# Causal mask of two attention units: added by VectorE in PSUM in place of two TensorE products

## The chip, the cores and the metric

The kernel runs on one core of a Trainium2 chip. The metric is the device time of one execution in microseconds (us). The median of three runs of the kernel before is 3585.42 us; the runs lie between 3579.69 and 3586.85.

## The reference

The program is two blocks of a network in float32, one after the other, on 512 tokens of width 1024. The first has two layers; each is a feed-forward part, a token mixer, and another feed-forward part. The mixer runs three kinds of attention side by side, all causal over blocks of 128 queries:

```python
s = jnp.einsum('bqhd,bkhd->bhqk', qn, k_nope) + ...          # mla: 4 heads
s = jnp.where(kpos[None, :] <= qpos[:, None], s, NEG)         # NEG = -1e30
p = jax.nn.softmax(s, axis=-1)
a = p[:, :, 0] - lam * p[:, :, 1]                             # diff: 4 heads, 2 maps each
o = gt[..., 0:1] * o_cmp + gt[..., 1:2] * o_slc + gt[..., 2:3] * o_win   # nsa: 8 heads
```

With 512 tokens the selected and the windowed attention of nsa both see all keys up to the query, so each of their maps is a plain causal softmax. The compressed attention has 31 keys and a mask of its own. The second block (retention, gated linear attention and two feed-forward parts) has no part in the change.

## The kernel before

Everything is written out by hand: one instruction stream for each of TensorE (`pe`), VectorE (`dve`), ScalarE (`act`), GpSimd (`pool`) and SyncE (`sp`), in the order of the code, with semaphores between them. A `signal` counts events of one kind; `x.wait_ge(*name(layer, n))` waits for the n-th.

Attention of a layer is 4 query tiles of 128 rows, handled in the order `TILE_AT = (3, 0, 2, 1)`. Tile 3 looks at four key tiles (512 keys), tile 0 at one, tile 2 at three, tile 1 at two. A tile has `UN` = 14 units, and a unit is two maps: 2 mla units, 4 diff units, 8 nsa units. So a layer has `NU` = 56 units and 112 maps. Each engine's `attention` runs over t, with i the place of the tile and `step` the unit in it. Work of several units overlaps: in round t,

- TensorE writes the scores of unit t (L3365) to two PSUM banks, one for each map. Two pairs of banks are used in turn, so it first waits for the exponentials of unit t-2. In diff and nsa units the two maps lie in different rows of the array; mla maps use 96 rows and come one after the other. Then it adds the mask: for each map one bf16 product of the identity `ident_b` with the triangle `causal_b` (0 or -1e30), accumulated on the last 128 columns (L3367). The event `scores_done` follows. Then come the transposes of the probabilities of unit t-3 (L3396), and the products of unit t-4 with the values (L3430 for the compressed part, L3437 for the rest).
- VectorE takes the maximum of both maps at once, negated, over all n columns (L2409, `max_ready`). It then copies the second transposed map of unit t-3 out of PSUM (L2418), and takes the reciprocal of the sums of unit t-1 (L2423).
- ScalarE copies the first transposed map of unit t-3 (L1448), waits for the maximum, and writes the exponentials of unit t with their sums (L1458).
- GpSimd scales the probabilities of a unit by the reciprocals (L958 to L962).

Some steps of each tile have more. At step 1 TensorE adds the compressed scores (L3375), and VectorE masks them and starts their softmax (`cmp_softmax`: L2362, L2366, L2368). At step 2 ScalarE takes their exponentials (L1464) and VectorE their sums (`cmp_sums`: L2374 to L2381). At step 6 their transposes follow (L3403). At steps 10 and 11 the diff outputs leave PSUM (L2442, L2443). In 18 of the 56 rounds TensorE also runs a piece of the second block's modulation, a product with `ada_w` (L3460). VectorE copies its rows at the end of the round (L2450), TensorE turns them in the next round behind the masks and before the transposes (L3383), and VectorE adds them to `mod` behind the reciprocal (L2428).

TensorE, VectorE and ScalarE each wait in order, so an instruction that waits holds up all behind it on its engine. `causal_b` is made once from `causal` and lies in SBUF.

Of the kernel before, what the change touches and what calls it, by code (L numbers as in the profile page):

```python
# [10 lines left out]
ALU = mybir.AluOpType  # L11
# [196 lines left out]
def build(nc, a, out):  # L208
    ctx = ExitStack()
    with ctx:  # L210
# [14 lines left out]
        def signal(name, per_layer, start=0):  # L225
            return Signal(sem(name), per_layer, start)
# [300 lines left out]
        gate_exp = signal("gate_exp", 1)  # L527
        gate_step = signal("gate_step", 2)
        scores_done = signal("scores_done", NU + TT)
        max_ready = signal("max_ready", NU)  # L530
        exp_ready = signal("exp_ready", NU)
        probs_turned = signal("probs_turned", 2 * NU)
        probs_t_act = signal("probs_t_act", NU)
# [493 lines left out]
        def _(act):  # L1027
# [403 lines left out]
            def attention(layer):  # L1431
# [6 lines left out]
                for t in range(NU + X_LAG):  # L1438
# [9 lines left out]
                        nc.scalar.activation(probs_t[u % 2][:, 0, 0:n], psum[:, 4, 0:n], ACT.Copy).then_inc(probs_t_act.sem, 1)  # L1448
                    if t < NU:

                        act.wait_ge(*max_ready(layer, t + 1))
                        tile = TILE_AT[i]
                        n = (tile + 1) * P
                        for m in range(2):
                            if m and u >= 0:

                                act.wait_ge(*probs_turned(layer, 2 * u + 2))
                            last = nc.scalar.activation(probs[:, t % 3, m, 0:n], psum[:, score_banks(t) + m, 0:n], ACT.Exp,  # L1458
                                                        bias=neg_max[:, 2 * t + m:2 * t + m + 1], accum_out=exp_sum[:, 2 * t + m:2 * t + m + 1])
                        last.then_inc(exp_ready.sem, 1)  # L1460
                        at = slice(tile * P, (tile + 1) * P)
                        if step == AT_CMP_EXP:
                            act.wait_ge(*cmp_step(layer, 2 + 7 * i + 3))
                            nc.scalar.activation(cmp_p[:, :, 0:NC], cmp_p[:, :, 0:NC], ACT.Exp).then_inc(cmp_exp.sem, 1)  # L1464
                        if step == AT_LAST and i:
                            last_high(i - 1)
                        if step == AT_FIRST:
                            act.wait_ge(*o_done(layer, i * UN + FIRST_NSA))
                            if i:

                                act.wait_ge(*diff_sum(layer, i))
                            nc.scalar.activation(diff_sq, psum[:, 6, 2 * P:4 * P], ACT.Square).then_inc(diff_squared.sem, 1)
                            nc.scalar.activation(h_hi[:, 0:2, at], psum[:, 6, 0:2 * P].rearrange("p (c q) -> p c q", c=2),
                                                 ACT.Copy).then_inc(o_hi_ready.sem, 1)
                        if step == AT_SUMS:
                            act.wait_ge(*diff_sum(layer, i + 1))
                            nc.scalar.activation(diff_sums(tile), psum[:, 6, 0:2 * P],
                                                 ACT.Copy, scale=-1.0).then_inc(diff_moved.sem, 1)
# [387 lines left out]
        def _(dve):  # L1866
# [525 lines left out]
            def attention(layer):  # L2392
# [11 lines left out]
                for t in range(NU + O_LAG + 1):  # L2404
                    i, step = divmod(t, UN)
                    if t < NU:
                        b = score_banks(t)
                        dve.wait_ge(*unit_scores_done(layer, t))
                        nc.vector.tensor_reduce(neg_max[:, 2 * t:2 * t + 2], psum[:, b:b + 2, 0:(TILE_AT[i] + 1) * P], AX_X, ALU.max,  # L2409
                                                negate=True).then_inc(max_ready.sem, 1)  # L2410
                    u = t - X_LAG
                    if 0 <= u < NU:
                        dve.wait_ge(*probs_turned(layer, 2 * u + 2))
# [494 lines left out]
        def _(pe):  # L2908
# [437 lines left out]
            def attention(layer):  # L3346
# [7 lines left out]
                for t in range(NU + O_LAG + 1):  # L3354
                    i, step = divmod(t, UN)
                    if t < NU:
                        if t >= 2:

                            pe.wait_ge(*exp_ready(layer, t - 1))
                        tile = TILE_AT[i]  # L3360
                        n = (tile + 1) * P
                        banks = [psum[:, score_banks(t) + m, :] for m in range(2)]
                        for m, head in enumerate(UNIT_MAPS[step]):
                            q, k, _ = key_values(*head)
                            nc.tensor.matmul(banks[m][:, 0:n], q(slice(tile * P, (tile + 1) * P)), k(n), start=True, stop=False)  # L3365
                        for m in range(2):
                            last = nc.tensor.matmul(banks[m][:, n - P:n], ident_b[:], causal_b[:], start=False, stop=True)  # L3367
                        last.then_inc(scores_done.sem, 1)
                        if step == AT_CMP:
                            if i:  # L3370

                                pe.wait_ge(*diff_moved(layer, i))
                                pe.wait_ge(*ada_read(layer, 2 * sum(at < t - 1 for at in ADA_STEPS)))
                            for c in range(NSA_H // NSA_G):
                                last = nc.tensor.matmul(psum[:, 6, 2 * c * CMP_BLOCK:2 * c * CMP_BLOCK + NSA_G * NC], q_nsa[:, c, tile * P:(tile + 1) * P],  # L3375
                                                        k_cmp[:].rearrange("p g n -> p (g n)"), start=True, stop=True)
                            last.then_inc(scores_done.sem, 1)
# [579 lines left out]
```

## Time and profile before

| | us |
|---|---|
| median of 3 runs | 3585.42 |
| runs | 3585.42, 3586.85, 3579.69 |
| span of the profiled execution | 3577.6 |
| TensorE busy | 3496.6 (98%) |
| TensorE weight loads busy | 2932.5 (82%) |
| VectorE busy | 1683.2 (47%) |
| ScalarE busy | 1484.3 (41%) |
| GpSimd busy | 1522.5 (43%) |
| masks (L3367) | 224 products per execution, 217 to 314 ns each |
| maxima (L2409) | 112, from 414 to 1226 ns |

The profile shows one execution. Its span runs from the first to the last instruction of the program, and a run's time lies some microseconds above it. PE is TensorE's products, PEld its weight loads, DVE is VectorE, ACT ScalarE, POOL GpSimd and SP SyncE. Products overlap each other, so each record is longer than the distance to the next, and a busy TensorE isn't one at its peak; the starts are what tells its pace. An arrow in a row names what ended an engine's idle time.

### The profile page before, as it was taken

The numbers are of one execution on the slowest core, as the hardware profiler recorded it, in microseconds if no ns is written. First come the engines' busy times: TensorE is split into PE (matmuls) and PEld (weight loads), VectorE is DVE, ScalarE is ACT, GpSimd is POOL, SyncE is SP. The second block draws the span as 40 slices with busy tenths as digits, with TensorE's granted clock in tenths as the row PEclk, the third lists the DMA queues.
The fourth block names the chain that finished last, engine by engine and source line by source line (L and its number), as shares of the span: only waits on it lengthen the run. The fifth ranks groups of instructions, "written<-read, shape, count | busy, mean of one in ns | idle before, by whom it ended". The sixth has DMA issues, their size and how long they took to land.

```text
span 3577.6 us, 56728 instructions
## 1 busy us (share of the span) xinstructions
PE 3496.6 (98%) x21603; PEld 2932.5 (82%) x21603; DVE 1683.2 (47%) x2814; ACT 1484.3 (41%) x2466; POOL 1522.5 (43%) x1352
## 2 busy tenths in 40 slices
PE   8999999999999999999999999999999999999998
PEld 7999776688998999776689997888888786778887
DVE  8456635575657565644575656211112504661112
ACT  5344434554545454534554545312112325443223
POOL 4555543445455554543435554323233532034443
PEclk9999999999999999999999999999999999999999
DMA  4343443323333343433314333222212323013332
GB/s 124 105 113 89 113 121 107 101 60 106 106 92 97 106 111 90 98 117 121 117 49 118 86 103 100 65 65 59 65 58 60 90 64 88 30 55 98 100 94 65
DMA packets 569573, 322.63 MB, mean 90 GB/s; under 512 B 30282, under 2 KB 563376, under 8 KB 569008
## 3 DMA queue, kind: packets, MB, share of 16 engines
q1 hardware_dynamic: 569392, 320.22, 31.4%
q8 instruction: 113, 1.85, 0.2%
q14 instruction: 68, 0.56, 0.1%
HBM read 318.08 MB, written 2.10 MB: 89 GB/s over the span
## 4 chain that ended last, share of the span: by engine, by line
PE 65%; issue 21%; POOL 8%; DVE 3%; ACT 1%; POOLq 0%; ACTq 0%; DVEq 0%
PE psum L3052 21%; PE psum L2945 16%; PE psum L3159 12%; POOL w_lo L945 7%; PE psum L3365 2%; PE psum L3437 2%; PE psum L3396 2%; PE psum L3339 1%; PE psum L3086 1%; PE psum L3089 1%; PE psum L3460 1%; PE psum L3206 1%; PE psum L3476 1%; PE psum L3367 1%; POOL set_lo L996 0%
## 5 line engine op out<-in xcount | busy, mean ns | idle before, releaser
L945 POOL TENSOR_TENSOR w_lo<-w_raw,w_hi 128x512 fp32r<-128x512 f32 x488 | 656.0, 1367 | 1107.9 <-ACT w_hi L1033 1107.9
L1033 ACT ACTIVATE w_hi<-w_raw 128x1024 fp32r<-128x1024 f32 x244 | 257.6, 1058 | 842.3 <-PE psum L2945 714.6
L2945 PE MATMUL psum<-h_hi,w_hi 128*128 128x512 f32 x1136 | 454.5, 400 | 1.4 <-POOL w_lo L945 1.4
L2945 PE MATMUL psum<-h_hi,w_lo 128*128 128x512 f32 x1136 | 447.2, 394 | 0.0
L2945 PE MATMUL psum<-h_lo,w_hi 128*128 128x512 f32 x1136 | 444.3, 391 | 0.0
L996 POOL TENSOR_TENSOR set_lo<-w_raw,set_hi 128x512 fp32r<-128x512 f32 x224 | 292.6, 1334 | 225.3 <-ACT set_hi L1112 222.3
L3052 PE MATMUL psum<-t_hi,set_hi 128*128 128x256 f32 x1280 | 363.4, 284 | 10.1 <-ACT gated L1102 8.2
L3052 PE MATMUL psum<-t_lo,set_hi 128*128 128x256 f32 x1280 | 362.4, 283 | 0.0
L3052 PE MATMUL psum<-t_hi,set_lo 128*128 128x256 f32 x1280 | 362.3, 283 | 0.0
L3159 PE MATMUL psum<-a_hi,set_hi 128*128 128x512 f32 x704 | 277.0, 393 | 2.8 <-DVE a_lo L2096 2.8
L3052 PE MATMUL psum<-b_hi,set_hi 128*128 128x256 f32 x960 | 272.6, 284 | 1.8 <-DVE gated L2168 1.8
L3159 PE MATMUL psum<-a_lo,set_hi 128*128 128x512 f32 x704 | 274.1, 389 | 0.0
L3159 PE MATMUL psum<-a_hi,set_lo 128*128 128x512 f32 x704 | 274.0, 389 | 0.0
L3052 PE MATMUL psum<-b_lo,set_hi 128*128 128x256 f32 x960 | 272.2, 284 | 0.0
L3052 PE MATMUL psum<-b_hi,set_lo 128*128 128x256 f32 x960 | 272.2, 284 | 0.0
L2945 PEld LDWEIGHTS psum<-h_hi,w_hi 128*128 128x128 f32 x1136 | 213.3, 188 | 60.5 <-issue 10.9
L978 POOL TENSOR_TENSOR set_lo<-w_raw,set_hi 128x512 fp32r<-128x512 f32 x160 | 212.6, 1349 | 114.9 <-ACT set_hi L1089 108.0
L2062 DVE TENSOR_TENSOR gated<-silu_g,psum 128x512 f32<-128x512 f32 x66 | 37.6, 597 | 474.8 <-ACT silu_g L1157 474.8
L984 POOL TENSOR_TENSOR set_lo<-w_raw,set_hi 128x512 fp32r<-128x512 f32 x160 | 210.9, 1339 | 114.8 <-ACT set_hi L1092 114.8
L3052 PEld LDWEIGHTS psum<-t_hi,set_hi 128*128 128x128 f32 x1280 | 245.8, 192 | 12.0 <-POOL set_lo L978 8.1
L2945 PEld LDWEIGHTS psum<-h_lo,w_hi 128*128 128x128 f32 x1136 | 213.3, 188 | 50.3 <-issue 4.3
L2945 PEld LDWEIGHTS psum<-h_hi,w_lo 128*128 128x128 f32 x1136 | 213.3, 188 | 45.9
(626 smaller groups left out, 8085.8 us busy)
## 6 DMA issues: line engine op xcount, KB each, us to landing
w_raw<-ffn_w SPq DMA_DIRECT2D x120, 512.0 KB, 3.8
w_raw<-ffn_w_gate SPq DMA_DIRECT2D x88, 512.0 KB, 4.0
w_raw<-ffn_w_up SPq DMA_DIRECT2D x88, 512.0 KB, 3.9
ada_raw<-ada_w SPq DMA_DIRECT2D x72, 512.0 KB, 4.7
w_raw<-ffn_w_down SPq DMA_DIRECT2D x64, 512.0 KB, 4.1
w_raw<-w_in SPq DMA_DIRECT2D x60, 512.0 KB, 3.8
w_raw<-ffn_w_down SPq DMA_DIRECT2D x32, 384.0 KB, 3.6
w_raw<-w_out SPq DMA_DIRECT2D x24, 512.0 KB, 4.1
```

Source lines behind the costliest of these rows:

```text
L945: last = nc.gpsimd.tensor_tensor(w_lo[:, i, at], w_raw[:, i, at], w_hi[:, i, at].bitcast(F32), ALU.subtract)
L978: last = nc.gpsimd.tensor_tensor(lo[:, at], w_raw[:, 2 * r, at], hi[:, at].bitcast(F32), ALU.subtract)
L984: last = nc.gpsimd.tensor_tensor(lo[:, to], w_raw[:, 2 * r + 1, at], hi[:, to].bitcast(F32), ALU.subtract)
L996: last = nc.gpsimd.tensor_tensor(set_lo[i // 2][:, to], w_raw[:, i, at], set_hi[i // 2][:, to].bitcast(F32), ALU.subtract)
L1033: nc.scalar.activation(w_hi[:, pos, :], w_raw[:, pos, :], ACT.Copy).then_inc(hi_ready, 1)
L2062: last = nc.vector.tensor_tensor(gated[:, i, o:o + n], silu_g[:, i, o:o + n], up, ALU.mult)
L2945: last = nc.tensor.matmul(dst, w[:, pos, k * P:(k + 1) * P], rhs[g][r](k0 + k), start=k == 0 and m == 0, stop=k == nk - 1 and m == 2)
L3052: last = nc.tensor.matmul(dst, w[r][:, at], x[:, k, cols], start=not onto and k == 0 and m == 0, stop=k == HALF_K - 1 and m == 2, skip_gro ...
L3159: last = nc.tensor.matmul(psum[:, 6 + i % 2, :], w[i // 2][:, at], x[:, k, :], start=k == m == 0, stop=k == nf - 1 and m == 2)
L3365: nc.tensor.matmul(banks[m][:, 0:n], q(slice(tile * P, (tile + 1) * P)), k(n), start=True, stop=False)
L3396: last = nc.tensor.transpose(psum[:, 4 + m, b * P:(b + 1) * P], probs[:, u % 3, m, b * P:(b + 1) * P], ident[:])
L3437: last = nc.tensor.matmul(o_place(kind, h), v(b), probs_t[u % 2][:, x, b * P:(b + 1) * P], start=first and b == 0, stop=final and b == TIL ...
```

## The change

For each unit VectorE adds the triangle to the last 128 columns of both banks in one instruction (128 partitions x 256 elements, `causal_b` repeated for both), reading and writing PSUM. It then waits for that result and takes the maximum. The events of both are counted in one signal, `max_step`, two for each unit; ScalarE waits for the second. TensorE no longer multiplies the identity with the triangle, and the scores of a map are one closed product. There are 112 additions more on VectorE, and 224 products and as many weight loads fewer on TensorE.

```diff
-        max_ready = signal("max_ready", NU)
+        max_step = signal("max_step", 2 * NU)
 ...
-                        act.wait_ge(*max_ready(layer, t + 1))
+                        act.wait_ge(*max_step(layer, 2 * t + 2))
 ...
                     if t < NU:
                         b = score_banks(t)
+                        n = (TILE_AT[i] + 1) * P
                         dve.wait_ge(*unit_scores_done(layer, t))
-                        nc.vector.tensor_reduce(neg_max[:, 2 * t:2 * t + 2], psum[:, b:b + 2, 0:(TILE_AT[i] + 1) * P], AX_X, ALU.max,
-                                                negate=True).then_inc(max_ready.sem, 1)
+                        diagonal = psum[:, b:b + 2, n - P:n]
+                        nc.vector.tensor_tensor(diagonal, diagonal, causal_b[:].rearrange("p (o k) -> p o k", o=1).broadcast_to([P, 2, P]),
+                                                ALU.add).then_inc(max_step.sem, 1)
+                        dve.wait_ge(*max_step(layer, 2 * t + 1))
+                        nc.vector.tensor_reduce(neg_max[:, 2 * t:2 * t + 2], psum[:, b:b + 2, 0:n], AX_X, ALU.max,
+                                                negate=True).then_inc(max_step.sem, 1)
 ...
                             q, k, _ = key_values(*head)
-                            nc.tensor.matmul(banks[m][:, 0:n], q(slice(tile * P, (tile + 1) * P)), k(n), start=True, stop=False)
-                        for m in range(2):
-                            last = nc.tensor.matmul(banks[m][:, n - P:n], ident_b[:], causal_b[:], start=False, stop=True)
+                            last = nc.tensor.matmul(banks[m][:, 0:n], q(slice(tile * P, (tile + 1) * P)), k(n), start=True, stop=True)
                         last.then_inc(scores_done.sem, 1)
```

## Rows read from the trace of the kernel before

**Rows 1.** The page, first part: busy time, share of the span, instructions.

```profile
PE 3496.6 (98%) x21603; PEld 2932.5 (82%) x21603; DVE 1683.2 (47%) x2814; ACT 1484.3 (41%) x2466; POOL 1522.5 (43%) x1352
```

**Rows 2.** Busy time by stretches: length, PE, PEld, DVE, ACT, POOL, clock, DMA, GB/s.

```profile
540.60:722.50 181.90, 172.68 (x1657) 111.85 (x1657) 98.30 (x251) 92.79 (x301) 71.92 (x118) 0.95 0.32 101
```

**Rows 3.** Waits of PE, 538 to 724 us: us in total, times, longest us.

```profile
PE psum L3430 <- DVE probs_t L2418: 2.4, 3, 0.9
PE psum L3437 <- DVE mod L2428: 2.2, 3, 0.9
PE psum L3383 <- DVE diff_rows L2450: 2.0, 2, 1.5
```

**Rows 4.** Timeline of PE: start us, us, line, operands, count [idle <- releaser].

```profile
545.49 0.28 PE L3367 MATMUL psum<-causal_b,ident_b 128*128 128x128 bf16 x2
545.60 1.05 PE L3375 MATMUL psum<-k_cmp,q_nsa 128*128 128x62 f32 x8
...
714.65 0.28 PE L3367 MATMUL psum<-causal_b,ident_b 128*128 128x128 bf16 x2
714.77 0.61 PE L3396 MATMUL psum<-ident,probs 128*128 128x128 f32 x4
...
719.41 0.66 PE L3396 MATMUL psum<-ident,probs 128*128 128x128 f32 x4
```

**Rows 5.** Single lines of DVE: count, ns min/median/max, first and last start, forms.

```profile
L2443 DVE TENSOR_TENSOR h_lo<-psum,h_hi x8: 414/415/415, 588.1 to 1795.6; 128x256 fp32r<-128x256 f32 x8
...
L2368 DVE TENSOR_TENSOR cmp_p<-cmp_p,cmp_stats x8: 416/506/864, 548.1 to 1769.7; 128x248 f32<-128x248 f32 x8
...
L2103 DVE TENSOR_TENSOR silu<-psum,silu x40: 414/425/426, 58.8 to 2153.9; 128x256 f32<-128x256 f32 x40
```

**Rows 6.** Timeline of DVE, tile 0.

```profile
622.20 0.42 DVE L2409 TENSOR_REDUCE neg_max<-psum 128x2 f32<-128x256 f32 x1 [0.58 <-PE psum L3367]
622.54 0.28 DVE L2418 COPY probs_t<-psum 128x128 f32<-128x128 f32 x1
...
623.43 0.42 DVE L2409 TENSOR_REDUCE neg_max<-psum 128x2 f32<-128x256 f32 x1 [0.54 <-PE psum L3367]
```

**Rows 7.** Timeline of DVE, steps 1 to 4 of tile 2.

```profile
638.41 0.41 DVE L2366 TENSOR_REDUCE cmp_stats<-cmp_p 128x8 f32<-128x248 f32 x1
638.85 0.42 DVE L2368 TENSOR_TENSOR cmp_p<-cmp_p,cmp_stats 128x248 f32<-128x248 f32 x1
639.19 0.95 DVE L2409 TENSOR_REDUCE neg_max<-psum 128x2 f32<-128x768 f32 x1
...
642.70 0.95 DVE L2409 TENSOR_REDUCE neg_max<-psum 128x2 f32<-128x768 f32 x1
...
644.11 0.40 DVE L2450 COPY diff_rows<-psum 128x256 f32<-128x256 f32 x1
...
645.92 0.56 DVE L2418 COPY probs_t<-psum 128x384 f32<-128x384 f32 x1 [0.55 <-PE psum L3396]
```

**Rows 8.** Timeline of ACT and PE: last exponential of a unit, scores two units on.

```profile
631.52 0.20 ACT L1458 ACTIVATION_READ_ACCUMULATOR probs<-psum,neg_max 128x1 f32 x1
...
632.39 0.91 PE L3365 MATMUL psum<-k_mla,q_mla 96*128 96x384 f32 x2
```

**Rows 9.** Timeline of PE, step 4 of tile 2.

```profile
644.57 0.61 PE L3383 MATMUL psum<-cond_sum,diff_rows 128*128 128x2 f32 x4 [0.57 <-DVE diff_rows L2450]
```

**Rows 10.** Timeline of DVE, step 2 of tile 3.

```profile
548.90 1.21 DVE L2409 TENSOR_REDUCE neg_max<-psum 128x2 f32<-128x1024 f32 x1
```

**Rows 11.** Timeline of DVE and PE, steps 3 and 4 of tile 1.

```profile
691.08 0.42 DVE L2450 COPY diff_rows<-psum 128x256 f32<-128x256 f32 x1 [0.35 <-PE psum L3460]
...
691.70 0.45 PE L3383 MATMUL psum<-cond_sum,diff_rows 128*128 128x2 f32 x3
```

**Rows 12.** Busy time by stretches, as rows 2: two stretches at half clock.

```profile
552.00:562.20 10.20, 8.83 (x46) 6.33 (x50) 5.16 (x12) 3.87 (x10) 2.58 (x4) 0.50 0.18 56
613.40:620.20 6.80, 6.56 (x43) 3.15 (x42) 2.84 (x9) 2.13 (x10) 2.18 (x5) 0.50 0.25 79
```

## The prediction, made before the changed kernel had run

> **What bounds the kernel now.** The page comes first: TensorE is busy 98% of the span [rows 1]. The change lies in two stretches, one per layer, between the first score matmul of attention and the first matmul of the output projection. The table by stretches gives 181.9 us for the first, with TensorE busy 172.7 and VectorE 98.3 [rows 2]; the second is as long. Then I read what TensorE waits for inside the first stretch: for VectorE in three places, 2.4 us in three waits behind the first transposes of the turn (L3430), 2.2 us in three waits before L3437, 2.0 us in two waits before L3383 [rows 3]. So TensorE sets the pace of most of the 56 units of a layer, and VectorE does so at a few fixed places. A saving on TensorE counts only in the first kind, a longer VectorE only in the second. These are read apart below.
>
> **Part 1, TensorE loses two bf16 matmuls a unit.** In a plain unit of two key tiles the masks start at 714.65 and the transposes behind them at 714.77: 0.12 us [rows 4]. That isn't all profit. Behind the masks the four transposes span 0.61 us, because their first weight load ran under a mask. At 719.41, where they follow matmuls that use the array in halves, as the scores of the diff and nsa units do, they span 0.66 [rows 4]. Without masks the transposes stand right behind such scores. So I take 0.12 - 0.05 = 0.07 us for a diff or nsa unit. In an mla unit the scores take turns on the whole array, the next weight load is prefetched anyway, and the masks cost all of 545.49 to 545.60, 0.11 us [rows 4]. Bounds: 0.12 for all (no exposed load), and zero (the pipe has to drain there whoever comes next).
>
> **Which units give it.** A layer has 8 mla and 48 other units. Units in which TensorE waits for VectorE give nothing: steps 1 to 3 of the first tile handled (queries of tile 3), 1 to 4 of the third (tile 2) and 1 to 4 of the fourth (tile 1), plus about two more at steps 10 and 11. That leaves 5 mla and 38 others: 5 x 0.11 + 38 x 0.07 = 3.2 us a layer.
>
> **Part 2, VectorE gets an add of 128x256 from and to PSUM, and a wait on itself.** The trace has no such add that writes to PSUM. Nearest is the subtraction at L2443, one input in PSUM, one in SBUF, the same size: 414 to 415 ns in all 8 [rows 5]. The wait costs more than it seems. Where nothing waits, the next instruction starts before the last has ended: the maximum at 622.20 takes 0.42 and the copy behind it starts at 622.54, after 0.34 [rows 6]. Where it waits for its predecessor's result, 638.41 with 0.41 is followed at 638.85, after 0.44 [rows 7]. I take 0.45 us from the start of the add to the start of the maximum. Bounds: 0.34 (no wait), and 0.86, the longest run of L2368, an instruction of about this size [rows 5]. Against that, the add can start before the masks would have ended: 0.22 us earlier (two masks of 0.28 us span, of which 0.06 passes while the scores drain) behind packed scores, 0.11 behind mla ones. The maximum then comes later by 0.45 - 0.22 = 0.23 us, or 0.34 in an mla unit.
>
> The Trainium skill ("VectorE: DVE Perf Modes", the section on the DRAIN) states that a semaphore after each VectorE instruction costs nothing extra over one after the last. By that rule the add costs 0.34, and the gain of the sum below would be 3.4 us instead of 1.5. The trace disagrees, with 0.44 against 0.34 between starts [rows 6, 7], so I go by the rows.
>
> **Where the later maximum is covered.** Queued behind it on VectorE are the copy of probs_t, the reciprocal, the ada add and copy. Who waits: ScalarE's exponential for the maximum, TensorE's transposes and outputs for the copy, GpSimd for the reciprocal. In most units the copy (L2418) waits for TensorE's transposes and not for the maximum: 645.92, after 0.55 us of idling [rows 7]. The exponential must end before the scores two units later; in about the tightest case they end at 631.72 and the scores start at 632.39, 0.67 left for 0.23 [rows 8]. In the narrow tile 0 (one key tile) the maxima stand 1.23 us apart, of which VectorE idles 0.54 [rows 6] and works 0.7. With the add it works 1.15 of some 1.17. That just fits, and is the thinnest cover here.
>
> **Where it isn't.** After step 1 of a tile VectorE does the compressed-attention softmax in one chain: maximum, softmax, maximum of step 2, exponentials, sums, maximum of step 3, copy of ada rows (L2450), for which TensorE's L3383 waits.
> - Tile 2: the maximum at 639.19 stands directly behind L2368, that at 642.70 behind the sums, the copy at 644.11 behind them [rows 7], and L3383 starts at 644.57 after idling 0.57 [rows 9]. Three adds lie in it; the first has a slack of 0.24 for its 0.34, so 0.10 + 0.45 + 0.45 = 1.0 us. The next add, behind that copy, fits the 0.55 before the copy.
> - Tile 3: the maximum of step 1 and that of step 2, at 548.90 right behind the softmax [rows 10], are in the chain of the 1.5 us wait [rows 3]: 0.34 + 0.45 = 0.79.
> - Tile 1: TensorE doesn't wait now; the copy starts at 691.08 after 0.35 of idling, ends at 691.50, and L3383 starts at 691.70 [rows 11], slack 0.20 + 0.35. Two adds, 0.90, less these 0.55: 0.35.
> - Tile 0: its ada copy waits for TensorE far longer than two adds take, and covers them.
> - Small: the wait for L2443 at step 11 of tile 3, 0.15; at the end the last unit's scaling on GpSimd, 0.2.
>
> **The sum.** 1.0 + 0.79 + 0.35 + 0.35 = 2.5 us lost per layer, 3.2 saved: 0.7 net, some 1.5 us for both. The profiled span is 3577.6; the median of the runs is 3585.4, 7.8 above it, the runs lie between 3579.7 and 3586.9, so what lies around the span is 2 to 9 us. 3577.6 - 1.5 = 3576.1 for the span, and the same step from the median gives 3583.9 us. A large edit, 448 instructions gone from TensorE, that nearly cancels.
>
> **Rivals.**
> 1. The masks' whole 0.12 us is won in every unit and the waits swallow nothing: 112 x 0.12 = 13.4 us, 3572; with today's waiting units left out 10 us, 3575. For it: TensorE's 98%. Against it: [rows 3], and 0.61 against 0.66 in [rows 4].
> 2. Slower: the add contends with GpSimd's scaling of probabilities for SBUF, in the same stretch. L2368 takes 416 to 864 ns [rows 5]; each add would take 0.44 us more. Per layer: 0.9 in tile 3, 1.3 each in tiles 2 and 1, 1.5 around steps 10 and 16 to 17, and 2.2 in the five back-to-back units of tile 0, where nothing covers it: some 7.3, 15 for both, 3585.4 - 1.5 + 15 = 3599 us. It decides from 0.26 us more per add ((7.2 + 1.5) / 15 x 0.44). Against it: L2103, PSUM with SBUF and the same size, stays at 414 to 426 ns in 40 instructions through stretches full of GpSimd work [rows 5].
> 3. The half clock. TensorE ran at half clock from 552.0 to 562.2 and from 613.4 to 620.2 in the first layer [rows 12], and once in the second; the first follows the waits at steps 2 and 3. One stretch of 6.8 us in which TensorE is busy 6.56 costs half of that, 3.3 us. The change adds 1.0 us and takes away the work of four units' masks just before L3383 in tile 2, so TensorE would idle 0.57 + 1.0 + 0.25 = 1.8 us there, as much as before the first stretch. One such stretch in each layer: +6.6 - 1.5, 3590.5. Three or more would be needed for slower by 0.2%. On the other side the one of 613.4 may vanish: 3580. The Trainium skill ("TensorE: Matmul & The Clock Gate", HAM oscillation) has the clock fall when waits break up the matmuls; by that rule these stretches come with longer waits, which is this rival.
> 4. The change doesn't do what it says: TensorE has to drain between scores and transposes, and the masks lay in that time. Nothing is saved and the 5 us of waits are paid: 3590.
>
> **Chances.** Forecast 0.48 (about 3580 to 3587), rival 1 0.16, rival 2 0.07, rival 3 with more half clock 0.13 and with less 0.08, rival 4 0.08. 0.2%, 7.2 us, is about what a measurement of this kernel can tell from no change: faster means under 3578.2, slower over 3592.6. Faster: rival 1 and a little of the others, 0.18. Slower: rival 2 and the far part of rival 3, plus chains longer than I see, 0.15. Within: 0.67. The range takes in the full mask saving with waits (3575) and more half clock with rival 4 (3594): 3574 to 3594.
>
> **What would show it.** Transposes start 0.00 to 0.01 us after the scores' last pass and the four of them span 0.66; the distance from the first score to the first score of the next unit shrinks by 0.07 in plain units (tiles 3, 2 and 1). The add takes 0.41 to 0.43 us, the maximum starts 0.45 after it. The waits of TensorE for L2450 grow from 2 to about 5 us per layer in tiles 3, 2 and 1; those before L3430 and L3437 stay at 0.6 to 0.95. The stretches of attention come out at 181 us each. I am wrong if the add takes over 0.5 us, if the plain units shrink by 0.12, or if the granted clock differs.

## The result, and the profile after

| | before | after |
|---|---|---|
| median, us | 3583.41 (9 runs, 3578.23 to 3586.85) | 3598.87 (9 runs, 3587.15 to 3603.66) |
| span of the profiled execution, us | 3577.6 | 3594.6 |
| mean granted clock in it | 0.993 | 0.987 |

The ratio is 1.0037, with a 95% interval of 1.0026 to 1.0048. The changed kernel is slower by 15.5 us, where 1.5 us less was forecast, and it lies outside the stated range of 3574 to 3594.

The page of the changed kernel, its busy times and the row of the clock over 40 slices of the span:

```profile
PE 3506.2 (98%) x21379; PEld 2930.0 (82%) x21379; DVE 1726.4 (48%) x2926; ACT 1486.8 (41%) x2466; POOL 1525.4 (42%) x1352
...
PEclk9999998999999999999899999999999999999999
```

Against [rows 1], TensorE has 224 instructions fewer and yet 9.6 us more busy time. That can't be its work. The clock row (the mean granted clock of each slice, in tenths) shows an 8 in two slices, and each lies in one of the two attention stretches. In the kernel before there is a 9 everywhere.

Busy time by stretches of the changed kernel (start:end, length, PE, PEld, DVE, ACT, POOL, clock, DMA share, GB/s; a clock of 0.50 is the lower of TensorE's two levels, 1.2 against 2.4 GHz, called half clock here): the first layer's attention, from its first score to the output projection, and four stretches in it.

```profile
538.50:730.00 191.50, 178.62 (x1545) 112.32 (x1546) 120.24 (x307) 93.99 (x301) 72.62 (x118) 0.89 0.30 95
549.80:560.00 10.20, 8.55 (x40) 6.07 (x40) 6.09 (x14) 4.16 (x11) 2.53 (x5) 0.50 0.19 62
611.20:624.90 13.70, 13.27 (x82) 6.77 (x78) 6.51 (x24) 4.94 (x25) 4.42 (x10) 0.50 0.30 98
628.30:638.50 10.20, 10.12 (x44) 5.27 (x45) 4.34 (x16) 3.81 (x17) 2.65 (x6) 0.50 0.04 13
652.20:659.00 6.80, 6.80 (x48) 3.93 (x44) 2.71 (x5) 2.32 (x8) 2.74 (x5) 0.50 0.01 2
```

The stretch that took 181.9 us at a clock of 0.95 [rows 2] takes 191.5 at 0.89, and that of the second layer 191.0 at 0.90; 181 each was forecast. The kernel before had two stretches at half clock in it, 10.2 and 6.8 us [rows 12]. Now there are four: 10.2 us in tile 3 as before, 13.7 us where 6.8 stood in tile 0, and two new ones, 10.2 us at the passage from tile 0 to tile 2 and 6.8 us in tile 2. In the second layer half-clock stretches in attention grew from 6.8 us to 37.5 (6.8, 13.7, 10.2 and 6.8). Over the whole profiled execution they add up to 97.8 us, against 54.7 before; attention has 78.4 of them, against 23.8. From the first score to the last unit's first score the two layers took 175.5 and 172.1 us before and take 184.8 and 184.0 now, 21.1 us more. Taken from unit to unit, these 21.1 us stand in ten units of each layer, those under the new or longer stretches: steps 5 to 9 of tile 0, its steps 11 to 13 with step 0 of tile 2, and step 5 of tile 2. They take 21.4 us more, and the 90 other distances together 0.3 less.

What TensorE waits for in the same stretch (us in total, times, longest us):

```profile
PE psum L3386 <- DVE diff_rows L2455: 5.0, 3, 2.5
PE psum L3433 <- DVE probs_t L2423: 2.5, 3, 1.0
PE psum L3440 <- DVE mod L2433: 2.2, 3, 0.9
```

These answer to [rows 3]. The wait for the copied ada rows grew from 2.0 to 5.0 us; the two others stay. The timeline of VectorE, then of TensorE, at steps 3 and 4 of tile 2:

```profile
647.33 0.42 DVE L2411 TENSOR_TENSOR psum<-psum,causal_b 128x256 f32<-128x256 f32 x1
647.79 0.96 DVE L2414 TENSOR_REDUCE neg_max<-psum 128x2 f32<-128x768 f32 x1
648.67 0.55 DVE L2423 COPY probs_t<-psum 128x384 f32<-128x384 f32 x1
649.13 0.15 DVE L2428 RECIPROCAL scaled_inv<-exp_sum 128x2 f32<-128x2 f32 x1
649.21 0.40 DVE L2455 COPY diff_rows<-psum 128x256 f32<-128x256 f32 x1
...
649.66 0.61 PE L3386 MATMUL psum<-cond_sum,diff_rows 128*128 128x2 f32 x4 [1.88 <-DVE diff_rows L2455]
```

The add stands in the chain, the maximum starts 0.46 us behind it, and TensorE idles 1.88 us where it idled 0.57 [rows 9]. The same wait in tile 3 is 2.5 us, and in tile 1 there is a new one of 0.56.

Two plain units of tile 1, TensorE in the kernel before, then TensorE and VectorE in the changed one:

```profile
714.02 0.70 PE L3365 MATMUL psum<-k_slc,q_nsa 64*128 64x256 f32 x4
...
716.12 0.70 PE L3365 MATMUL psum<-k_win,q_nsa 64*128 64x256 f32 x4
...
721.24 0.70 PE L3370 MATMUL psum<-k_slc,q_nsa 64*128 64x256 f32 x4
721.88 0.66 PE L3399 MATMUL psum<-ident,probs 128*128 128x128 f32 x4
...
723.27 0.70 PE L3370 MATMUL psum<-k_win,q_nsa 64*128 64x256 f32 x4
...
721.99 0.43 DVE L2411 TENSOR_TENSOR psum<-psum,causal_b 128x256 f32<-128x256 f32 x1 [0.76 <-PE psum L3370]
722.46 0.69 DVE L2414 TENSOR_REDUCE neg_max<-psum 128x2 f32<-128x512 f32 x1
```

The transposes follow the scores directly and span 0.66 us, and the distance from score to score is 2.03 us. It was 2.10 in the kernel before, from 714.02 to 716.12.

### The profile page after: what moved, and what is told of

Read it like the earlier page. It is cut to its first block, busy times and chain, and to the rows that moved or that the text cites. A ratio compares the mean times of both kernels' runs of the same rounds, so it can differ in the third digit from the quotient of the medians.

```text
span 3594.6 us, 56392 instructions
## 1 busy us (share of the span) xinstructions
PE 3506.2 (98%) x21379; PEld 2930.0 (82%) x21379; DVE 1726.4 (48%) x2926; ACT 1486.8 (41%) x2466; POOL 1525.4 (42%) x1352
## 4 chain that ended last, share of the span: by engine, by line
PE 64%; issue 22%; POOL 8%; DVE 3%; ACT 1%; POOLq 0%; ACTq 0%; DVEq 0%
PE psum L3057 21%; PE psum L2950 16%; PE psum L3164 12%; POOL w_lo L945 7%; PE psum L3370 2%; PE psum L3440 2%; PE psum L3399 2%; PE psum L3344 1%; PE psum L3463 1%; PE psum L3091 1%; PE psum L3094 1%; PE psum L3211 1%; PE psum L3479 1%; PE psum L3386 0%; POOL set_lo L996 0%
## 5 line engine op out<-in xcount | busy, mean ns | idle before, releaser
L2062 DVE TENSOR_TENSOR gated<-silu_g,psum 128x512 f32<-128x512 f32 x66 | 37.5, 596 | 474.8 <-ACT silu_g L1157 474.8
```

What stands on the lines that cost most here:

```text
L2062: last = nc.vector.tensor_tensor(gated[:, i, o:o + n], silu_g[:, i, o:o + n], up, ALU.mult)
```

## How the clock is taken apart from the rest

A single run's time swings with its clock, so I give each run two numbers: its time, and its half-clock time, (1 - mean clock) x 2 x span. The mean clock has three digits, which makes steps of 7 us. The changed kernel has 101 us of half clock in the median (79 to 115), the kernel before 64 (36 to 79, 98 runs beside the experiments, median time 3583.5). This number covers the whole execution: in the 14 profiled ones 19 to 46 us of it lie outside attention.

A least-squares fit through all 223 runs of all kernels below, with one level for each kernel and one common slope, leaves a scatter of 1.4 us. Its slope is 0.37 us of time for 1 us at half clock. The last column of the table is the kernel's level against the kernel before: what it would cost or gain if the clock were the same (uncertain by about 0.5 us, the scatter over the root of the runs). The four groups of runs of the kernel before, taken beside the experiments on three chips, differ by up to 1.1 us by the same reckoning, so differences of 1 us between kernels of different groups mean little. The limit of 90 us in the table was chosen after the runs were seen.

| kernel | runs | median, us | ratio to before (95%) | half clock, us | runs over 90 us of it | at equal clock, us |
|---|---|---|---|---|---|---|
| before | 98 | 3583.5 | | 64 | 0 | 0 |
| after | 9 | 3598.9 | 1.0037 (1.0026 to 1.0048) | 101 | 7 | +0.1 |
| e1_both | 10 | 3591.4 | 1.0025 (1.0015 to 1.0035) | 65 | 0 | +8.4 |
| e2_neither | 10 | 3578.1 | 0.9986 (0.9976 to 0.9996) | 72 | 1 | -7.6 |
| e3_tile0_on_pe | 10 | 3586.9 | 1.0006 (0.9997 to 1.0016) | 79 | 0 | -0.1 |
| e4_mixed | 10 | 3579.0 | 0.9992 (0.9981 to 1.0002) | 64 | 0 | -4.7 |
| e5_tile0_twice | 10 | 3588.6 | 1.0013 (1.0003 to 1.0023) | 72 | 0 | +0.9 |
| e6_tile0_bare | 10 | 3589.8 | 1.0017 (1.0007 to 1.0027) | 83 | 4 | -1.0 |
| e7_filled_waits | 10 | 3581.2 | 1.0003 (0.9983 to 1.0024) | 64 | 3 | -1.6 |
| e9_before_filled | 10 | 3576.4 | 0.9978 (0.9966 to 0.9991) | 46 | 0 | -0.6 |
| e10_fill_tile2 | 10 | 3587.4 | 1.0021 (1.0001 to 1.0040) | 86 | 4 | -2.5 |
| e11_fill_tile3 | 10 | 3582.5 | 0.9999 (0.9986 to 1.0012) | 64 | 1 | -1.2 |
| e8 and e12 together | 16 | 3572.8 | (each for itself, below) | 50 | 0 | -4.8 |

The theory after the result: the sum of waits and savings is right, and the loss is half clock. Its rival: the adds cost more than they seem to in some place, and the clock only goes along with it.

## Experiments: the two halves of the change

The diffs are shortened to two functions: `adds(t)` says whether VectorE adds the mask of unit t, and `products(t)` whether TensorE forms its mask products. In the changed kernel they are True and False.

**e1_both.** TensorE's products stay, VectorE adds as well.

```diff
-    products(t): return False
+    products(t): return True
```

> TensorE keeps its two mask products in every unit and VectorE adds the triangle as well (masked twice, which changes nothing in the result): the VectorE half of the change alone. Theory A, that the half clock in the narrow tile 0 comes from the two products missing on TensorE: tile 0 goes as in the kernel before (first layer one stretch of half clock or none, not 13.7 + 10.2 us), and only the waits behind VectorE are paid: 3583.4 + 5 = 3588, up to 3595 if the longer wait in tile 2 (step 4) still brings a stretch of half clock in each layer. Theory B, that the half clock comes from VectorE's add, which makes everything behind it later: half clock as in the changed kernel, and the masks' time on top: 3605.

**e2_neither.** Neither of them; the causal mask is left out.

```diff
-    adds(t): return True
+    adds(t): return False
```

> No mask products on TensorE and no add on VectorE: the TensorE half of the change alone (the causal mask of these units is left out, so the result is another). Theory A: half clock in tile 0 of both layers as in the changed kernel (23.9 us of it per layer there), but not the stretch behind step 4 of tile 2, whose wait is short again: 3599 less 5 of waits less 5 to 6 of clock, 3588. Theory B: half clock as in the kernel before, and the saving of 0.07 to 0.15 us a unit counts: 3583.4 - 8.6 = 3575.

Measured: 3591.4 and 3578.1 us. At equal clock the adds alone cost 8.4 us, and the products alone are worth 7.6. e1 came out as theory A had it (3588 to 3595). e2 lies between its two theories (3588 and 3575), nearer to B: with the products gone and nothing added, nine of ten runs stayed at 86 us of half clock or less. In e1 TensorE's wait for the copied rows is 3.7 us in all, longest 1.9. Its half clock is at the level of the kernel before, and in its profiled execution tile 0 has none. The windows (first row tile 0, second row tile 2):

```profile
611.20:624.90 13.70, 12.14 (x126) 7.32 (x122) 9.38 (x33) 7.14 (x34) 5.95 (x14) 1.00 0.57 181
644.30:651.10 6.80, 6.80 (x48) 4.27 (x50) 2.62 (x5) 2.52 (x8) 2.93 (x5) 0.50 0.00 0
```

In the window of tile 0 that ran at 0.50 in the changed kernel the clock is 1.00 here, although VectorE adds there too; tile 2 has its stretch of 6.8 us. In e2, with nothing added, one run in ten fell to 100 us of half clock. It is the profiled one, and it has 13.7 us of it in tile 0:

```profile
611.80:625.50 13.70, 13.28 (x80) 6.94 (x80) 4.66 (x18) 4.39 (x24) 4.36 (x10) 0.50 0.29 88
```

The same 13.7 us stand in its second layer; another 46 us of its 104 lie outside attention. So tile 0 can fall without any add. The two halves sum to +0.8 us; together, in the changed kernel and its three filled versions below, they give +0.1 to -2.5. A likely reason is one that the prediction used: with the products gone the add starts earlier. No run separates it.

**e3_tile0_on_pe.** The change in tiles 3, 2 and 1 only.

```diff
-    adds(t): return True
-    products(t): return False
+    adds(t): return t // UN != 1
+    products(t): return t // UN == 1
```

> The change in tiles 3, 2 and 1; in tile 0 (the second handled, 14 units a layer) the masks stay TensorE products and VectorE adds nothing. Theory A: tile 0 and the start of tile 2 lose their half clock, which cost 4.8 + 1.6 us in the first layer and 7.3 + 1.6 in the second by the distances between scores: 3598.9 - 15 = 3584. The stretch behind step 4 of tile 2 (2.7 us a layer) stays. Theory B, waits of tile 2 and 3 that bring the clock down: little changes, 3595 to 3599.

Measured: 3586.9 us, 79 us of half clock, no run over 79. Theory A had 3584, theory B 3595 to 3599. 12 of the 15 us of the loss are gone with tile 0's change undone, and at equal clock nothing moved (-0.1). Tile 2 still has its stretch (645.0 us, 10.2 us long) behind a wait of 1.9.

**e4_mixed.** As e3, and steps 1 to 3 of every tile also keep the products, so the softmax chain has no add in it. 33 of 56 units add on VectorE.

```diff
+    adds(t): return t // UN != 1 and not 1 <= t % UN <= 3
+    products(t): return not adds(t)
```

> As the one before, and steps 1 to 3 of every tile keep their mask products too, so that VectorE has no add in the chain of the compressed softmax. 33 units of 56 add on VectorE. Theory A, with the waits as a second and separate cost: no half clock beyond that of the kernel before, TensorE's waits for the ada copy back at 2 us a layer, and the saving of 30 x 0.075 + 3 x 0.14 = 2.7 us a layer: 3583.4 - 5.3 = 3578. Theory B (any add brings half clock): 3590 or more.

Measured: 3579.0 us (3578 by theory A), 64 us of half clock, -4.7 at equal clock. The waits for the copied rows and the clock in the window in which tile 2 fell in the changed kernel:

```profile
PE psum L3399 <- DVE diff_rows L2465: 1.7, 2, 0.9
...
644.00:654.00 10.00, 8.78 (x88) 5.79 (x89) 6.93 (x16) 5.55 (x16) 4.73 (x8) 1.00 0.53 169
```

With the wait in tile 2 back to 0.8 us its stretch is gone. But tile 0 fell in this execution (13.7 us from 610.1), with its products in place and no add.

## Experiments: what sends tile 0 down

**e5_tile0_twice.** The change, and in tile 0 the products as well.

```diff
-    products(t): return False
+    products(t): return t // UN == 1
```

> The change as it is in every tile, and in tile 0 TensorE forms the two mask products of a unit as well (the mask is added twice there, which leaves the probabilities as they are). VectorE and its waits are those of the change; TensorE has its 14 x 2 products of tile 0 back. Theory W (tile 0 falls to half clock because work of TensorE is missing there, so that small waits weigh more): tile 0 stays at full clock as in the kernel before, or falls in some runs only; the stretches of tile 2 behind the wait for diff_rows stay as in the changed kernel; half-clock time a run 65 to 80 us, time 3588 +-3 (changed kernel 3599, less 20 to 30 us of half clock at 0.4 us per us). Theory A (it is the add on VectorE that makes tile 0 fall, whatever TensorE does): tile 0 falls as in the changed kernel, half-clock time about 100 us, 3597 to 3601.

**e6_tile0_bare.** The change in tiles 3, 2 and 1; in tile 0 neither, so its causal mask is left out.

```diff
-    adds(t): return True
+    adds(t): return t // UN != 1
```

> The change in tiles 3, 2 and 1; in tile 0 neither the products nor the add (the causal mask of tile 0 is left out, so the result differs there). Theory W: the products are missing as in the changed kernel, so tile 0 falls to half clock in most runs, about 95 to 105 us of half clock a run and 3595 to 3599. Theory A: without the add tile 0 stays at full clock, half-clock time 65 to 80 us and 3586 +-3. A mixture (products gone alone: some runs, as in the kernel without mask and add, where 3 of 10 runs had over 75 us) would give a median at 3586 to 3590 with a wide spread.

Measured: e5 3588.6 us and 72 us of half clock, no run over 86. Theory W gave 3588, theory A 3597 to 3601: the add isn't what makes tile 0 fall. e6 3589.8 us, with runs at 79 to 115 us of half clock, four of ten over 90. That is the mixture named in advance, not W's "most runs". The profiled run of e6 is one of those four, and shows how far a fall can reach:

```profile
612.40:626.10 13.70, 13.45 (x82) 6.76 (x80) 4.85 (x19) 4.83 (x25) 4.42 (x11) 0.50 0.31 100
629.40:666.90 37.50, 36.61 (x174) 20.50 (x174) 16.92 (x46) 13.59 (x48) 10.85 (x19) 0.50 0.10 34
```

The pairs that differ in tile 0's products alone say the same: over 90 us of half clock in 7 of 9 executions of the changed kernel and in 0 of 10 of e5, in 4 of 10 of e6 and 0 of 10 of e3. So does the whole set, 20 of 59 executions of the six kernels without the products in tile 0 (after, e2, e6, e7, e10, e11) and none of 164 of those that have them (before, e1, e3, e4, e5, e8, e9, e12), though these kernels differ in their waits too. The missing products in tile 0 open the way to the executions with much half clock; they don't force one, and e4 shows that a single 13.7 us fall can come with the products in place.

## Experiments: do the waits send the clock down?

These kernels put products that nobody reads into a wait of TensorE, just ahead of it: 128 bf16 columns of the identity with `causal_b`, into bank 4, which is free there. They do nothing but keep TensorE at work.

```diff
+                    if FILL.get(t):
+                        if t > X_LAG:
+                            pe.wait_ge(*first_turn_read(layer, TURN_AT["unit", t - X_LAG] - 1))
+                        for _ in range(FILL[t]):
+                            nc.tensor.matmul(psum[:, 4, 0:P], ident_b[:], causal_b[:], start=True, stop=True)
                     if t - 1 in ADA_AT:
```

**e7_filled_waits.** The change with `FILL = {3: 30, 32: 26}`, tile 3's step 3 and tile 2's step 4.

> The change, with products that nobody reads (128 columns of bf16 into a free bank) in TensorE's two longest waits for diff_rows: 30 of them in tile 3's step 3 (the wait there is 2.5 us) and 26 in tile 2's step 4 (1.9 us), where they end before the awaited rows are there. Nothing else moves. Theory I (the idle stretch itself sends the clock down behind it): the half-clock stretches at 549.8/10.2 us and 652.2/6.8 us, and their two of the second layer, are gone, the half-clock time falls by 20 to 34 us to 65 to 80 us, and the time by 8 to 14 us to 3585 to 3591. If the clock falls for what TensorE does over a longer time, or by something outside of the wait, the stretches stay and the time stays at 3597 to 3601. Tile 0 isn't touched: its stretches stay under theories W and A; only if tile 0's fall follows on tile 3's is it gone too.

Measured: 3581.2 us, 17.6 less than the changed kernel (12.8 between the means), for 56 products a layer that compute nothing. Half clock in the median is 64 us, down from 101. Theory I had 3585 to 3591; the rest of the gain is tile 0's, which fell less often. Against the kernel before it isn't faster (1.0003). The timeline of TensorE at step 3 of tile 3, and the windows of the stretches:

```profile
549.24 1.85 PE L3399 MATMUL psum<-causal_b,ident_b 128*128 128x128 bf16 x30
551.61 0.61 PE L3405 MATMUL psum<-cond_sum,diff_rows 128*128 128x2 f32 x4 [0.53 <-DVE diff_rows L2466]
...
549.80:560.00 10.20, 9.67 (x101) 6.73 (x100) 8.03 (x18) 4.91 (x13) 3.85 (x6) 1.00 0.39 119
610.00:620.20 10.20, 10.20 (x70) 5.32 (x66) 4.23 (x15) 3.28 (x17) 3.17 (x8) 0.50 0.34 104
652.20:659.00 6.80, 6.80 (x69) 4.30 (x67) 4.74 (x12) 3.65 (x11) 2.60 (x4) 1.00 0.50 147
```

The 30 products fill the wait, the awaited rows still come later, and 0.53 us of idling is left. Where the changed kernel ran at 0.50 from 549.8 and from 652.2, this one runs at 1.00. Tile 0 still fell once, in the first layer; the second layer has no half clock in attention at all. Against the rival after the result: that layer has the same adds in tile 0, and steps 6 to 9 take 8.8 us from score to score, where the changed kernel took 13.7 at half clock and the kernel before 8.4. Three of the ten runs have 108 us of half clock, so the tile 0 falls aren't cured.

**e10_fill_tile2** and **e11_fill_tile3.** One fill alone: `FILL = {32: 26}` and `FILL = {3: 30}`.

> The change with only the wait of tile 2's step 4 filled (26 unread products). Theory I: its two stretches of 6.8 us go and nothing else changes: 3599 - 14 x 0.4 = 3593 +-3, half-clock time 87 us, tile 0 (which comes before) as in the changed kernel. If tile 2's stretch was not caused by this wait: 3597 to 3601.

> The change with only the wait of tile 3's step 3 filled (30 unread products). Theory I in its narrow form (a wait reaches only the stretch right behind it): the stretches at 549.8/10.2 and 1648.9/6.8 go, 3599 - 17 x 0.4 = 3592 +-3, tile 0 and tile 2 as in the changed kernel. In a wider form (tile 0 falls because tile 3 fell before it): tile 0's stretches go in many runs as well, half-clock time 50 to 65 us, time 3578 to 3585.

Measured: e10 3587.4 us with 86 us of half clock (87 expected), and the first layer of its profile has the stretches of tiles 3 and 0 as in the changed kernel, while the window of tile 2 runs at full clock:

```profile
549.70:559.90 10.20, 8.51 (x40) 6.07 (x40) 6.09 (x14) 4.20 (x11) 2.54 (x5) 0.50 0.18 58
611.20:624.90 13.70, 13.27 (x82) 6.78 (x79) 6.46 (x24) 4.93 (x24) 4.42 (x10) 0.50 0.28 92
644.00:654.00 10.00, 8.77 (x91) 5.56 (x88) 7.20 (x19) 5.25 (x16) 4.50 (x7) 1.00 0.34 108
```

The time came out 6 us below the 3593 expected. Four of its runs lie at 108 to 122 us of half clock and six at 64 to 86, so a median of ten is a coarse number here. e11 gave 3582.5 us with 64 us of half clock, what the wide form said: only one run of ten went over 90, against seven of nine in the changed kernel. But e7, which has the same fill, had three of ten. Together, over 90 us came in 4 of 20 executions with tile 3's wait filled (e7, e11) and in 11 of 19 without (after, e10). That what happens in tile 3 reaches tile 0, 50 us later, is suggested by this and not settled, and how it would isn't shown. Nor do the falls of tile 3 all vanish: in the profile of e11 one of 6.8 us still stands at 552.5 and one of 3.4 in the second layer.

**e9_before_filled.** The kernel before in its order of work (masks on TensorE), with `FILL = {3: 20}`.

> The kernel before in its order of work (masks on TensorE, none on VectorE) with 20 unread products in its longest wait for diff_rows, tile 3's step 3 (1.5 us in the first layer, 1.8 in the second). If the idle stretch sends the clock down whatever the mask does, the stretches at 552.0/10.2 and 1640.8/6.8 us go: half-clock time 64 - 17 = 47 us, time 3584 - 7 = 3577 +-3, and the changed kernel with its waits filled (3581, median 64 us of half clock) has then to be set beside that. If filling helps only where VectorE adds the mask, it stays at 3584.

Measured: 3576.4 us, ratio 0.9978 (0.9966 to 0.9991), 46 us of half clock, where 3577 and 47 were expected. In its profile the two windows of [rows 12] are at full clock. In the second layer, though, it fell in tiles 0 and 2 (the last two rows), without any wait over 0.9 us close ahead of either:

```profile
552.00:562.20 10.20, 10.20 (x99) 6.50 (x97) 5.74 (x13) 6.00 (x16) 5.12 (x7) 1.00 0.36 115
613.40:620.20 6.80, 5.98 (x66) 3.70 (x64) 3.82 (x15) 4.00 (x19) 2.89 (x7) 1.00 0.72 234
...
1688.50:1695.30 6.80, 6.55 (x42) 3.18 (x40) 2.77 (x9) 2.17 (x10) 2.18 (x5) 0.50 0.22 73
1722.60:1729.40 6.80, 6.80 (x46) 3.62 (x42) 2.28 (x4) 1.90 (x6) 2.38 (x4) 0.50 0.00 0
```

So the mechanism isn't bound to where the mask is added. It was in the kernel before, and the change fed it.

**e8_mixed_filled** and **e12_mixed_again.** e4 with `FILL = {3: 18, 32: 10}`; the same kernel twice.

> The mixed kernel of before (VectorE's add in tiles 3, 2 and 1 but for their steps 1 to 3, TensorE's products elsewhere; 3579.0 us, 64 us of half clock) with unread products in the same two waits, 18 in tile 3's step 3 and 10 in tile 2's step 4. Theory I: the stretch that follows tile 3's step 3 in each layer (10.2 and 6.8 us) is gone, half-clock time about 48 us, time 3579 - 6 = 3573 +-3. If the wait doesn't send the clock down: 3579 as without them, or 1 us more if 18 products reach past the wait.

> The mixed kernel with the two filled waits once more, unchanged, since it was executed only four times and is the fastest so far. If its gain is that of the shorter waits and the stretches that went, it stays at 3569 +-3 with a half-clock time of 29 to 50 us; if the four runs were a lucky draw of tile 0, single runs come at 65 to 80 us of half clock and the median moves to 3573 to 3578. The kernel before stays at 3584.

Measured: e8 3568.6 us in four runs, ratio 0.9950 (0.9933 to 0.9967). e12 3576.5 us in twelve runs on another chip, 0.9992 (0.9979 to 1.0005), half clock from 36 to 86 us. The first was a lucky draw, as e12's second case had it. The sixteen together have a median of 3572.8, between 3567.0 and 3588.4, 10.7 us under the 3583.5 of the kernel before. Beside its own group of the kernel before (3580.8) e12 alone is 4.3 us lower. At equal clock the kernel stands where e4 stands, at -4.8. It is the fastest tried, but only one of its two groups is clear of no change. Of the kernels that compute the whole mask, the one that beats the kernel before with a clear interval in a group of ten is e9.

**All profiled executions together**, two layers of each of 14. The wait is that of TensorE for the copied rows, as it stands or as the fill leaves it:

| | wait, us | layers | with a half-clock stretch behind it |
|---|---|---|---|
| tile 3, step 3, not filled | 0.9 to 2.5 | 18 | 18 (6.8 or 10.2 us) |
| tile 3, step 3, filled | 0 to 0.6 | 10 | 3 (3.4 to 6.8 us) |
| tile 2, step 4, not filled | 1.7 to 1.9 | 11 | 11 (6.8 or 10.2 us) |
| tile 2, step 4, not filled, neither mask nor add (e2) | 0.9 | 2 | 2 |
| tile 2, step 4, short or filled | 0 to 0.8 | 14 | 1 |

Left out is the first layer of e6, whose 37.5 us cover tile 2 already. For tile 2 the question is settled: a wait of 1.7 to 1.9 us sends the clock down, and unread products in it keep it up. A second wait there, 0.87 us for `mod`, comes some 2 us later in all these kernels, and doesn't do it alone.

In tile 3 the wait for the copied rows isn't the only one that counts. Some 2 us ahead of it TensorE waits 0.7 to 2.2 us for the weights `ada_w` from DMA, and in three of the 18 layers (one each of e3, e5 and e10) the half clock began 1.0 to 1.8 us before the wait for the rows had begun, right behind a wait for `ada_w` of 1.45 to 1.58. In e5's second layer, TensorE's timeline and the window from 1638.6:

```profile
1637.71 0.64 PE L3476 MATMUL psum<-ada_raw,cond 128*32 128x256 f32 x8 [1.45 <-DMA ada_raw<-ada_w]
1638.28 1.79 PE L3380 MATMUL psum<-k_diff,q_diff 32*128 32x512 f32 x4
1641.43 1.02 PE L3399 MATMUL psum<-cond_sum,diff_rows 128*128 128x2 f32 x4 [1.36 <-DVE diff_rows L2465]
...
1638.60:1648.80 10.20, 8.84 (x36) 5.21 (x34) 5.92 (x13) 4.65 (x14) 2.78 (x4) 0.50 0.28 92
```

With the wait for the rows filled, the three layers that still fell had waits for `ada_w` of 1.4, 2.1 and 2.2 us; six with 0.8 to 1.2 us, and one with 1.46, stayed up. So filling the wait for the rows helps there, and a wait for DMA of 1.4 us or more can do the same harm. For tile 0 the cause isn't settled.

Filling tile 0 as well wasn't tried: the bank that could take the products is being read by ScalarE at that time.

## Why the prediction was wrong, step by step

**Part 1** holds. Transposes behind the scores span 0.66 us, plain units shrink by 0.07 (2.10 to 2.03 in tile 1, 3.40 to 3.33 in tile 3), most mla units by 0.11 to 0.17 where 0.11 was taken. Steps 1 to 3 of tile 1, which were counted as giving nothing, shrink as well. The products alone are worth 7.6 us for both layers (e2), where 6.4 was said.

**Part 2** holds. The add takes 408 to 433 ns where 414 was taken, in all 56 of a layer, and the maximum starts 0.44 to 0.47 us after it. The Trainium skill ("VectorE: DVE Perf Modes", the section on the DRAIN) has a semaphore cost nothing extra, from which the prediction had estimated 0.34 us. The trace disagrees again.

**Where it isn't covered** holds as well, in the main. L3386's waits came to 5.0 us ("about 5"), the wait of tile 2 to 1.88 us (0.57 plus 1.0 plus 0.25 was said), the new one of tile 1 to 0.56 (0.35), and step 11 of tile 3 lost 0.31 (0.15). The waits before the other two lines stayed. One place was missed: tile 0. That it "just fits" can be read in e7's second layer, which runs at full clock. From step 5 on its units take what they took before or up to 0.08 us less, but step 6 takes 3.64 us where 3.10 stood. VectorE comes late out of an instruction of 0.69 us for another part (L2407), the add stands behind it, and TensorE waits 0.28 us for the copy behind both, where it didn't wait before:

```profile
1694.09 0.69 DVE L2407 TENSOR_TENSOR h_lo<-psum,h_hi 128x512 fp32r<-128x512 f32 x1 [0.96 <-ACT h_hi L1445]
1694.69 0.42 DVE L2422 TENSOR_TENSOR psum<-psum,causal_b 128x256 f32<-128x256 f32 x1
...
1695.49 0.28 DVE L2434 COPY probs_t<-psum 128x128 f32<-128x128 f32 x1
...
1695.83 0.33 PE L3418 MATMUL psum<-ident,probs 128*128 128x128 f32 x1 [0.28 <-DVE probs_t L2434]
```

**The sum**, -1.5 us, fits only at equal clock, and there to 1 or 2 us: +0.1 for the changed kernel, -1.2 to -2.5 for its three filled versions, a mean of -1.3 over 39 runs. That it comes so near is in part luck, since a saving taken too small (6.4 against 7.6) and the wait missed in tile 0 pull against each other.

**The step that failed** is one the sum never wrote down: that TensorE's granted clock stays as it was. It took the kernel before's half clock as given and added waits to it. The runs have 36 us more half clock in the median (101 against 64), and at 0.37 us each this is some 13.5 us. By the means it closes: 3596.9 us of the changed kernel against 3583.2 of the 98 runs of the kernel before is 13.8 more, and 37 us more half clock give 13.6 of them. The medians lie 15.5 apart, but nine runs make a coarse one. The prediction had named a differing clock among the signs of being wrong, but its sum had no term for it.

**Rival 3** had the mechanism, and tile 2's place and wait (1.8 us said, 1.88 found, one stretch of 6.8 us in each layer). It was given 0.13, because I looked for falls only behind a wait made longer. It said that three or more stretches would be needed to be slower by 0.2%, and didn't ask where the others could come from. They came in tile 0 and at its end: 13.7 and 10.2 us in each layer of the profiled execution, where [rows 12] already showed that this tile is near the edge (6.8 us in one layer, none in the other). Two things go with it: its products were gone (over 90 us in 7 of 9 executions, in 0 of 10 of e5, where they are back), and perhaps that tile 3's wait was longer (4 of 20 against 11 of 19). I had read the cover of tile 0 as a question of VectorE's time only. The price was too high: 3.3 us for a stretch of 6.8, where about 3.1 was lost at step 4 and 5 of tile 2, and 4.9 for 13.7.

**Rival 2** (GpSimd) fell: no add took more than 433 ns. That its 3599 us is what was measured is chance. **Rival 1** fell with the 0.07 of the plain units, and **rival 4** too, since the products' absence is worth 7.6 us.

## What to carry to other kernels

Where the profile of a kernel shows half-clock stretches behind waits of TensorE, its time has a term that no sum of instructions contains. List these stretches and the waits ahead of them, and ask of every edit whether it takes work from TensorE near one or makes a wait ahead of one longer, a wait for DMA included; give that case its own price for each place, and a chance to match. And try the cheap cure first: products that nobody reads in the longest waits, which won 8.5 us beside the kernel before (e9) and 17.6 between medians in the changed one (e7).

## What the runs showed of the hardware

- Waits of TensorE for the copied rows of 1.7 to 2.5 us had 6.8 to 10.2 us at half clock behind them every time, which began in the wait or up to 2.5 us after it; with 26 to 30 products in them the clock stayed at 1.00 (e7, and tile 2 in e10). The shorter waits decide nothing by themselves: behind 0.9 us tile 2 fell in both layers of e2, behind 0.8 in none of e4. Waits for DMA count like those for VectorE: behind 1.45 to 1.58 us for `ada_w` the clock fell in three layers before the next wait came.
- TensorE can be busy nearly all the time and still run at half clock: 13.27 of 13.7 us, 36.61 of 37.5. Its busy share doesn't tell what is lacking, since its records are longer at half clock.
- The same kernel falls in some executions and not in others: the changed kernel has 79 to 115 us of half clock, e7 36 to 108, and its times run from 3571.9 to 3600.8 us. One execution of each of two kernels decides nothing here unless the clock is read beside the time.
- A microsecond at half clock cost 0.37 us over all runs, not the half that I had taken. The Trainium skill ("TensorE: Matmul & The Clock Gate", HAM oscillation) reckons the penalty as half of the throttled time. Estimated by that, the 36 us more would be 18 us; the fit gives 13.5. Stretch by stretch, by the distances between scores in the second layer against e7, which has no half clock there, 13.7 us cost 4.9, 10.2 cost 4.3 and 6.8 cost 3.1, or 0.36 to 0.46 us each. Waiting explains a part at 549.8 (8.55 us of 10.2 were busy), but the three were busy for 97% and more, so why they cost less than half isn't shown.
- The same page ("A second HAM failure mode: psum-queue depth-cycling") has the clock oscillate where TensorE idles often and briefly between groups of products. Tile 0 looks like it: its fall at 611.2 follows a wait of 0.60 us for `mod`, with none longer close ahead, and e9's second layer fell there likewise. But that wait stands in every kernel, fallen or not, and no run here shows that the small waits are the cause.
